# Eight small products side by side: state queries of a retention stage over four column tiles

## The chip, the cores and the metric

The kernel runs on one core of a Trainium2 chip. The metric is the time of one execution on the device in microseconds (us), the median of the runs shown. The engines in this document are TensorE (PE; its weight loads are listed apart as PEld), VectorE (DVE), ScalarE (ACT), GpSimd (POOL, which here mostly issues DMAs), and the queue of SyncE (SP), which issues the other DMAs.

## The reference, cut to what matters

One inference step of two decoder layers, for a prompt of 256 tokens and for a sample group of 8 batch entries with 4 tokens each. The second layer is a retention layer with 4 heads, keys of 256 and values of 512 elements. For the sample group each batch entry has a carried state of 4 heads x 256 x 512, which is read, used and written back:

```python
def retention_block(q, k, v, s_prev, log_g):
    ...
    o = jnp.einsum('bhij,bjhe->bihe', scores, v)
    q_decay = jnp.exp(log_g[None, :] * (i[:, None] + 1.0))
    o = o + jnp.einsum('bihd,bhde->bihe', q, s_prev) * q_decay[None, :, :, None]
    ...
    s_new = jnp.exp(log_g * L)[None, :, None, None] * s_prev + jnp.einsum('bjhd,bjhe->bhde', k * k_decay[None, :, :, None], v)
    return o, s_new
```

The second line of `o` is the query of the state (q times `s_prev`), and `s_new` is its update. The prompt goes through the same block in two chunks of 128 tokens for each head.

## The kernel before, in words

The retention stage has eight units. Unit n does two things at once. For the prompt it does head h = n // 2, chunk c = n % 2. For the sample group it does batch entry b = n: all of that entry's states, 2 MB, which are eight blocks (k = 0 to 7; head k // 2, half k % 2 of the 256 key rows) of 128 partitions x 512 values.

The program order is written out by hand for each engine, with semaphores between the engines. On PE (`pe_odd`) a unit is: the prompt's scores (into bank 5); state blocks 0 and 1; the S products of the prompt's key and value (banks 0 and 1); state blocks 2 and 3; scores times V (bank 6), and where c = 1 two more products with `qd` and S1; state blocks 4 to 7; and the four transposes of `rn`, for which PE waits until DVE has written `rn`. A state block (`sample_states`) is two products: the query, in which 32 columns of `QM` (the queries of all heads' sample tokens, zero outside this batch entry) meet the block and add to the 32 partitions of head h in bank 4 (`BN`), at column tile (0, 32 h); and the state product of `K4m` and `V4`, over the whole array, into bank 2 or 3 in turn. DVE then updates the block in place (`update`: decay times old state plus that bank).

On DVE a unit is: the scores' decay (`scr`), `qd` where c = 1, the gating of the unit before, updates 0 and 1, a rounding step of the unit before, updates 2 and 3, the two S2 steps where c = 1, update 4, the moments of bank 6, update 5, the reciprocal and the scaled rows (`rn`), and updates 6 and 7. ACT does a root between the moments and the reciprocal.

The states lie in the four slots of the weight ring `raw`, two to a batch entry (heads 0 and 1, heads 2 and 3, 1 MB each). So a slot goes round every two units: POOL stores half of entry n after update 3 or 7 (line 584), and the half of S2 where c = 1 (line 587); SP, whose queue is in order, waits for that store and loads the same half of entry n + 2 (line 303). PE waits for the half that a query reads (`SR_in`). When the stage is over PE goes on to the output projection, whose operands hang on the last `rn`.

The same column tiles are used in two other places: line 1179, four products of 512 columns ahead of the stage, one on each tile, and line 1268, the sample scores of cross-attention, eight products of 256 columns on four tiles.

Of the kernel before, what the change touches and what calls it, by code (L numbers as in the profile page):

```python
# [24 lines left out]
SEQ, DEC_B, DEC_T = 256, 8, 4  # L25
NS = DEC_B * DEC_T
# [10 lines left out]
RH, RDK, RDV = 4, 256, 512  # L37
# [26 lines left out]
def build(nc, a, outs):  # L64
# [31 lines left out]
    with ctx:  # L96
        def sb(name, shape, dt=F32, scope=ctx):
            return scope.enter_context(nc.sbuf_tensor(name, [P] + shape, dt))

        def sem(name):  # L100
            return ctx.enter_context(nc.semaphore(name))
# [98 lines left out]
        QM = sb("QM", [8, DEC_B * (NS + DEC_T)], F32, od)  # L200
# [25 lines left out]
        def state_slot(b, hp):  # L226


            return (G["out", 1].first + 2 + 2 * (b % 2) + hp) % 4

        def state(b, h):
            return raw[:, state_slot(b, h // 2), 4 * (h % 2):4 * (h % 2) + 4, :].rearrange("p (d x) n -> p d (x n)", d=2)
# [11 lines left out]
        ps = ctx.enter_context(nc.psum_tensor("ps", [P, 8, 512], F32))  # L244
        BN = 4
# [10 lines left out]
        def s(name):  # L256
            if name not in S:
                S[name] = sem(name)
            return S[name]
# [295 lines left out]
        def transpose(pe, out, x, rows=P):  # L555
            return pe.transpose(out, x, ident[0:rows, 0:rows])  # L556
# [305 lines left out]
        def dve_odd(dve, l):  # L862
# [77 lines left out]
            def update(b, k):  # L940

                dve.wait_ge(s("SU_ps"), 8 * b + k + 1)
                st = state(b, k // 2)[:, k % 2, :]
                dve.scalar_tensor_tensor(out=st, in0=st, scalar=gL(k // 2, DEC_T), in1=ps[:, 2 + k % 2, :],  # L944
                                         op0=ALU.mult, op1=ALU.add).then_inc(s("SR_new"), 1)
# [180 lines left out]
        def pe_odd(pe, l):  # L1126
            g = G["in", l]
            first_step(pe, g, 3 * l, normed, s("z_ready"), CREDIT)
            products(pe, g, normed, s("z_ready"), CREDIT, i0=1, i1=4)

            def naturals(i, idx):

                if idx or i == 4:
                    return
                for t in range(4):
                    e = 4 * (i - 5) + t
                    pe.wait_ge(s("v4T_ready"), e + 1)
                    if e >= 2:
                        pe.wait_ge(s("vR_ready"), e - 1)
                    bank = 5 + e % 2  # L1140
                    for c in range(2):
                        transpose(pe, ps[:, bank, c * P:(c + 1) * P], vt[:, t, c * P:(c + 1) * P])
                    transpose(pe, ps[:, bank, 2 * P:3 * P], v4T[:, t, :, :].rearrange("p r i -> p (r i)")).then_inc(s("vR_ps"), 1)
            for i in range(4, 9):
                products(pe, g, normed, s("z_ready"), CREDIT, i0=i, i1=i + 1, hook=naturals)

            products(pe, g, normed, s("z_ready"), CREDIT, i0=9, i1=10)
            pe.wait_ge(s("kdup"), 1)
            for h in range(RH):
                for dt in range(2):  # L1150
                    mm = pe.matmul(ps[0:64, 7, h * NS:(h + 1) * NS], k4T[:, 2 * h + dt, 0:2, :].rearrange("p r i -> p (r i)"),
                                   mT[:, 2 * h + dt, SEQ:T], start=dt == 0, stop=dt == 1)
            mm.then_inc(s("scS_ps"), 1)
            products(pe, g, normed, s("z_ready"), CREDIT, i0=10, i1=11)
            pe.wait_ge(s("k4T_full"), 1)
            pe.wait_ge(s("vR_ready"), 16)
            for r in range(2):
                for k in range(4):
                    tr = transpose(pe, ps[:, 5 + r, k * P:(k + 1) * P], k4T[:, 4 * r + k, :, :].rearrange("p r i -> p (r i)"))
                tr.then_inc(s("k4_ps"), 1)  # L1160

            def turn_keys(n):
                c, hf = divmod(n, 2)
                for k in range(4):
                    tr = transpose(pe, ps[:, KR_BANKS[n], k * P:(k + 1) * P], sq[:, 4 * hf + k, c * P:(c + 1) * P])
                tr.then_inc(s("kR_ps"), 1)

            def before_heads(i, idx):


                if idx:
                    return
                pe.wait_ge(s("K4_ready"), 2)
                pe.wait_ge(s("scS_ready"), 1)
                for n in range(3):
                    turn_keys(n)
                pe.wait_ge(root_ready, 2 * 3 * l + 1)
                for h in range(RH):
                    pe.matmul(ps[h * NS:(h + 1) * NS, BN, :], scS[0:64, h, :], V4[0:64, h * RDV:(h + 1) * RDV].bitcast(F32),
                              start=True, stop=False, skip_group_check=True, tile_position=(0, h * NS))  # L1180
            products(pe, g, normed, s("z_ready"), CREDIT, i0=11, i1=12, hook=before_heads)
            pe.wait_ge(s("kR_ready"), 3)
            turn_keys(3)

            def sample_states(b, tiles):

                for k in tiles:
                    h = k // 2
                    n = 8 * b + k
                    pe.wait_ge(s(f"SR_in{b % 2 * 2 + h // 2}"), 16 * (b // 2) + 16)  # L1190
                    pe.matmul(ps[h * NS:(h + 1) * NS, BN, :], QM[:, k, b * NS:(b + 1) * NS], state(b, h)[:, k % 2, :], start=False,  # L1191
                              stop=b == DEC_B - 1 and k % 2 == 1, skip_group_check=True, tile_position=(0, h * NS))
                    if k == 0:
                        pe.wait_ge(s("K4m_ready"), b + 1)
                    if n >= 2:
                        pe.wait_ge(s("SR_new"), n - 1)
                    pe.matmul(ps[:, 2 + k % 2, :], K4m[:, b % 2, k * P:(k + 1) * P], V4[:, h * RDV:(h + 1) * RDV],  # L1197
                              start=True, stop=True).then_inc(s("SU_ps"), 1)

            pe.wait_ge(s("z_ready"), CREDIT + 48)  # L1200
            pe.wait_ge(s("QM_step"), 3)

            for n, (h, c) in enumerate(UNITS):
                tok = slice(c * CHUNK, (c + 1) * CHUNK)
                if n:
                    pe.wait_ge(s("rs_ready"), n)
                for dt in range(2):
                    mm = pe.matmul(ps[:, 5, 0:P], sq[:, 2 * h + dt, tok], mT[:, 2 * h + dt, tok], start=dt == 0, stop=dt == 1)
                mm.then_inc(s("rs_ps"), 1)
                sample_states(n, (0, 1))  # L1210

                if n:
                    if c == 1:
                        pe.wait_ge(s("S1_ready"), h + 1)
                    else:
                        pe.wait_ge(s("S2_ready"), 2 * h)
                for dt in range(2):
                    pe.matmul(ps[:, dt, :], kR[:, c, h * RDK + dt * P:h * RDK + dt * P + P], vR[:, c, h * RDV:(h + 1) * RDV],
                              start=True, stop=True).then_inc(s("S_ps"), 1)
                sample_states(n, (2, 3))  # L1220
                pe.wait_ge(s("rs_ready"), n + 1)
                if n:
                    pe.wait_ge(s("rn_ready"), n)
                pe.wait_ge(s("kR_ready"), 4)
                mm = pe.matmul(ps[:, 6, :], scr[:, n % 2, :], vR[:, c, h * RDV:(h + 1) * RDV], start=True, stop=c == 0)
                if c == 1:
                    pe.wait_ge(s("qd_ready"), h + 1)
                    pe.wait_ge(s("S1_ready"), h + 1)
                    for dt in range(2):
                        mm = pe.matmul(ps[:, 6, :], qd[:, dt, :], S1[:, dt, :], start=False, stop=dt == 1)  # L1230
                mm.then_inc(s("ro_ps"), 1)
                sample_states(n, (4, 5, 6, 7))
                pe.wait_ge(s("rn_ready"), n + 1)
                if n:
                    pe.wait_ge(s("rg_ready"), n)
                for k in range(4):
                    tr = transpose(pe, ps[:, 7, k * P:(k + 1) * P], rn[:, k * P:(k + 1) * P])
                tr.then_inc(s("rT_ps"), 1)
            pe.wait_ge(s("rn_ready"), 9)
            pe.wait_ge(s("rg_ready"), 8)  # L1240
            for k in range(4):
                tr = transpose(pe, ps[:, 7, k * P:(k + 1) * P], rn[:, k * P:(k + 1) * P])
            tr.then_inc(s("rT_ps"), 1)
# [660 lines left out]
```

## Time and profile before

| what | value |
|---|---|
| median of 3 runs | 1332.78 us (1331.82 to 1333.16) |
| span of the profiled execution | 1330.2 us, from the first to the last instruction |
| PE busy | 1230.3 us, 92% of the span |
| DVE busy | 768.5 us, 58% |
| ACT busy | 584.4 us, 44% |
| moved by DMA | 233.64 MB, mean 176 GB/s |
| mean granted TensorE clock | 0.971 of full |

The profiled execution has no time of its own beside its span; the span lies 2.6 us below the median. Busy time is the sum of the instructions' durations without overlap, and matmuls that run together in one array count once. Durations of single instructions include the way through the array, so the start of the next instruction tells better what one costs.

### The profile page before, as it was taken

What the parts mean: (1) busy time and instruction counts of PE and PEld (TensorE: products, weight loads), DVE (VectorE), ACT (ScalarE), POOL (GpSimd) and SP (SyncE); (2) the same over time, 40 slices, a digit from 0 to 9 for tenths busy, and PEclk for the clock granted to TensorE, in tenths of its full rate; (3) what the DMA queues carried; (4) which work ended last, traced back from release to release, by engine and by line L of the source; (5) the groups of instructions that cost most, each with busy time, mean ns of one, the idle gap of its engine ahead of it and who ended that gap; (6) DMA issues with size and microseconds to landing.
All of it is one profiled execution on the core that took longest, in us unless ns stands there. A gap on an engine that the chain in (4) does not pass through costs nothing. (4 is left out here: it accounts for less than half of the span.)

```text
span 1330.2 us, 22925 instructions
## 1 busy us (share of the span) xinstructions
PE 1230.3 (92%) x8557; PEld 1091.7 (82%) x8557; DVE 768.5 (58%) x1020; ACT 584.4 (44%) x940; POOL 294.2 (22%) x521
## 2 busy tenths in 40 slices
PE   6999998887999999799999999899998779999995
PEld 4999897587999999699996333599996579999994
DVE  3585735227888733866555665447445167888433
ACT  5456534235655644423345111155434156556442
POOL 4001201114556510200000111003001125564402
PEclk9999999998999999799999999899999789999998
DMA  9647555632545355354444777748647324444440
GB/s 215 234 131 255 188 190 197 251 103 83 171 158 166 126 163 193 105 173 148 142 158 155 272 284 279 255 147 284 226 154 253 138 95 159 158 159 146 150 127 36
DMA packets 177267, 233.64 MB, mean 176 GB/s; under 512 B 5374, under 2 KB 153226, under 8 KB 177200
## 3 DMA queue, kind: packets, MB, share of 16 engines
q1 hardware_dynamic: 159088, 169.09, 39.2%
q0 software_dynamic: 18112, 63.60, 13.6%
q8 instruction: 48, 0.79, 0.2%
q14 instruction: 19, 0.16, 0.0%
HBM read 207.50 MB, written 25.16 MB: 175 GB/s over the span
## 5 line engine op out<-in xcount | busy, mean ns | idle before, releaser
L392 PE MATMUL ps<-hh,wh 128*128 128x288 f32 x1600 | 486.3, 304 | 34.8 <-DVE hl L450 28.2
L327 DVE TENSOR_TENSOR wl<-raw,wh 128x2048 fp32r<-128x2048 f32 (+2 forms) x154 | 331.7, 2154 | 313.4 <-ACT wh L324 313.3
L392 PE MATMUL ps<-hl,wh 128*128 128x288 f32 x1600 | 478.9, 299 | 0.0
L392 PE MATMUL ps<-hh,wl 128*128 128x288 f32 x1600 | 477.0, 298 | 0.0
L324 ACT ACTIVATE wh<-raw 128x2048 fp32r<-128x2048 f32 (+3 forms) x154 | 277.7, 1804 | 296.5 <-PE ps L392 288.0
L392 PEld LDWEIGHTS ps<-hh,wh 128*128 128x128 f32 x1600 | 306.1, 191 | 41.6 <-issue 33.8
L392 PEld LDWEIGHTS ps<-hh,wl 128*128 128x128 f32 x1600 | 308.0, 192 | 0.0
L392 PEld LDWEIGHTS ps<-hl,wh 128*128 128x128 f32 x1600 | 307.5, 192 | 0.3
L392 PE MATMUL ps<-aH,wh 128*128 128x288 f32 x352 | 104.2, 296 | 0.0
L392 PE MATMUL ps<-aL,wh 128*128 128x288 f32 x352 | 103.8, 295 | 0.0
L392 PE MATMUL ps<-aH,wl 128*128 128x288 f32 x352 | 103.6, 294 | 0.0
L458 POOL TENSOR_TENSOR mT<-mT,rstd 128x288 f32<-128x288 f32 x42 | 40.8, 1004 | 227.7 <-DVE rstd L433 227.7
L392 PE MATMUL ps<-wh,mh 128*128 128x256 f32 x256 | 73.4, 287 | 6.0 <-DVE wl L327 6.0
L584 POOL DMA_DIRECT2D out<-raw x16 | 12.2, 761 | 284.4 <-DVE raw L944 284.4
L392 PE MATMUL ps<-wl,mh 128*128 128x256 f32 x256 | 72.4, 283 | 0.0
L392 PE MATMUL ps<-wh,ml 128*128 128x256 f32 x256 | 72.4, 283 | 0.0
L944 DVE SCALAR_TENSOR_TENSOR raw<-raw,ps 128x512 f32<-128x512 f32 x64 | 43.6, 682 | 46.3 <-PE ps L1197 46.3
L1455 POOL TENSOR_TENSOR aL<-pd,aH 128x288 f32 (+1 forms) x44 | 68.6, 1578 | 4.2 <-ACT aH L1581 4.2
L1191 PE MATMUL ps<-raw,QM 128*32 128x512 f32 x128 | 66.9, 605 | 0.0
L392 PEld LDWEIGHTS ps<-aH,wl 128*128 128x128 f32 x352 | 66.3, 188 | 0.0
L392 PEld LDWEIGHTS ps<-aL,wh 128*128 128x128 f32 x352 | 66.1, 188 | 0.0
L392 PEld LDWEIGHTS ps<-aH,wh 128*128 128x128 f32 x352 | 66.0, 187 | 0.0
(286 smaller groups left out, 1682.3 us busy)
## 6 DMA issues: line engine op xcount, KB each, us to landing
raw<-w_ffn_up SPq DMA_DIRECT2D x44, 1024.0 KB, 5.0
raw<-w_in_odd SPq DMA_DIRECT2D x24, 1024.0 KB, 5.1
ring<-cache_mem_k POOLq DMA_DIRECT2D x16, 1024.0 KB, 5.4
ring<-cache_mem_v POOLq DMA_DIRECT2D x16, 1024.0 KB, 6.2
raw<-state_retention SPq DMA_DIRECT2D x16, 1024.0 KB, 5.2
out<-raw POOLq DMA_DIRECT2D x16, 1024.0 KB, 5.3
raw<-w_ffn_down SPq DMA_DIRECT2D x16, 768.0 KB, 4.4
raw<-w_in_even SPq DMA_DIRECT2D x10, 1024.0 KB, 6.7
```

The costliest lines, as they stand in the source:

```text
L324: e.activation(wh[:, c % 2, 0:kn, :], src, ACT.Copy).then_inc(hi_ready, 1)
L327: e.tensor_tensor(wl[:, c % 2, 0:kn, :], src, wh[:, c % 2, 0:kn, :].bitcast(F32), ALU.subtract).then_inc(lo_ready, 1)
L392: mm = pe.matmul(out, lhsT, rhs, start=(kc == 0 and n_k == 0 and n == 0), stop=(kc == g.nk - 1 and n_k == kn - 1 and n == 2))
L458: pool.tensor_tensor(mT[:, t, :], mT[:, t, :], rstd[:], ALU.mult).then_inc(scaled, 1)
L584: pool.dma_start(states_dram(ret_sample, n, half), states(n, half)).then_inc(s(f"SR_out{n % 2 * 2 + half}"), 16)
L944: dve.scalar_tensor_tensor(out=st, in0=st, scalar=gL(k // 2, DEC_T), in1=ps[:, 2 + k % 2, :], op0=ALU.mult, op1=ALU.add).then_inc(s("SR_ne ...
L1191: pe.matmul(ps[h * NS:(h + 1) * NS, BN, :], QM[:, k, b * NS:(b + 1) * NS], state(b, h)[:, k % 2, :], start=False, stop=b == DEC_B - 1 and ...
L1455: pool.tensor_tensor(aL[:, i * 2 + j, :], pd[:, j, :], aH[:, i * 2 + j, :].bitcast(F32), ALU.subtract).then_inc(s("a_lo"), 1)
```

## The change

A new helper issues the eight queries of a batch entry together, at the start of the unit, just behind the prompt's scores: first half 0 of the key rows for the four heads, one on each column tile, then half 1. PE waits for both halves of the entry's states ahead of them. The queries, and their waits, leave `sample_states`, which keeps the state products where they were. Update 0 of an entry waits on DVE for the last of the queries (`SQ_ps`), since it overwrites what they read.

```diff
             def update(b, k):
                 dve.wait_ge(s("SU_ps"), 8 * b + k + 1)
+                if k == 0:
+                    dve.wait_ge(s("SQ_ps"), b + 1)
...
+            def sample_rows_of(b):
+                for hp in range(2):
+                    pe.wait_ge(s(f"SR_in{b % 2 * 2 + hp}"), 16 * (b // 2) + 16)
+                for dt in range(2):
+                    for h in range(RH):
+                        k = 2 * h + dt
+                        mm = pe.matmul(ps[h * NS:(h + 1) * NS, BN, :], QM[:, k, b * NS:(b + 1) * NS], state(b, h)[:, dt, :], start=False,
+                                       stop=b == DEC_B - 1 and dt == 1, skip_group_check=True, tile_position=(0, h * NS))
+                mm.then_inc(s("SQ_ps"), 1)
...
                 for k in tiles:
                     h = k // 2
                     n = 8 * b + k
-                    pe.wait_ge(s(f"SR_in{b % 2 * 2 + h // 2}"), 16 * (b // 2) + 16)
-                    pe.matmul(ps[h * NS:(h + 1) * NS, BN, :], QM[:, k, b * NS:(b + 1) * NS], state(b, h)[:, k % 2, :], start=False,
-                              stop=b == DEC_B - 1 and k % 2 == 1, skip_group_check=True, tile_position=(0, h * NS))
...
                 mm.then_inc(s("rs_ps"), 1)
+                sample_rows_of(n)
                 sample_states(n, (0, 1))
```

## Rows read from the trace of the kernel before

**Rows 1.** The page, engines: busy us, share of the span, instructions.

```profile
PE 1230.3 (92%) x8557; PEld 1091.7 (82%) x8557; DVE 768.5 (58%) x1020; ACT 584.4 (44%) x940; POOL 294.2 (22%) x521
```

**Rows 2.** Stretches: the stage, a c = 0 unit, a c = 1 unit, each from rn to rn.

```profile
core 0: us, PE busy (x) PEld busy (x) DVE busy (x) ACT busy (x) POOL busy (x), PEclk, DMA share, GB/s
719.40:842.10 122.70, 122.70 (x311) 37.96 (x311) 73.34 (x130) 21.75 (x30) 14.22 (x19) 1.00 0.75 268
779.90:794.50 14.60, 14.60 (x39) 4.50 (x38) 8.34 (x16) 2.99 (x4) 1.53 (x2) 1.00 0.81 288
794.50:810.90 16.40, 16.40 (x43) 5.27 (x42) 9.96 (x20) 1.96 (x3) 2.21 (x3) 1.00 0.79 287
```

**Rows 3.** Groups of the stage by line: busy us, mean ns, idle before.

```profile
L1191 PE MATMUL ps<-raw,QM 128*32 128x512 f32 x128 | 66.9, 605 | 0.0
```

**Rows 4.** Timeline into a unit: start us, us, engine, line, operation.

```profile
780.40 0.50 PE L1197 MATMUL ps<-V,K4m 128*128 128x512 f32 x1
...
780.93 0.69 DVE L944 SCALAR_TENSOR_TENSOR raw<-raw,ps 128x512 f32<-128x512 f32 x1 [0.55 <-PE ps L1197]
...
781.71 1.05 PE L1191 MATMUL ps<-raw,QM 128*32 128x512 f32 x2
...
782.69 0.50 PE L1197 MATMUL ps<-V,K4m 128*128 128x512 f32 x1
```

**Rows 5.** Timeline of PE in a c = 1 unit, scores times V.

```profile
803.34 0.51 PE L1197 MATMUL ps<-V,K4m 128*128 128x512 f32 x1
803.68 1.02 PE L1225 MATMUL ps<-vR,scr 128*128 128x512 f32 x2
804.54 1.88 PE L1230 MATMUL ps<-S,qd 128*128 128x512 f32 x4
806.35 1.04 PE L1191 MATMUL ps<-raw,QM 128*32 128x512 f32 x2
```

**Rows 6.** Timeline of DVE in a c = 0 unit, from update 4 on.

```profile
791.50 0.69 DVE L944 SCALAR_TENSOR_TENSOR raw<-raw,ps 128x512 f32<-128x512 f32 x1 [1.65 <-PE ps L1197]
...
793.70 0.81 DVE L1021 TENSOR_SCALAR rn<-ps,small 128x512 f32<-128x512 f32 x1
```

**Rows 7.** Timeline of PE at lines 1179 and 1268, with what follows each.

```profile
710.58 1.06 PE L1179 MATMUL ps<-V,rowsn 64*32 64x512 f32 x8
711.57 0.40 PE L392 MATMUL ps<-hh,wh 128*128 128x288 f32 x1
...
1023.35 1.09 PE L1268 MATMUL ps<-kTb,qB 128*32 128x256 f32 x16
1024.37 0.48 PE L1284 MATMUL ps<-prT,vN 128*128 128x256 f32 x1
```

**Rows 8.** Timeline of DVE in unit 0: updates 0 and 1, update 4.

```profile
723.45 1.28 DVE L944 SCALAR_TENSOR_TENSOR raw<-raw,ps 128x512 f32<-128x512 f32 x2
...
729.22 0.69 DVE L944 SCALAR_TENSOR_TENSOR raw<-raw,ps 128x512 f32<-128x512 f32 x1 [1.65 <-PE ps L1197]
```

**Rows 9.** DMA issues (KB, us to landing), two in the timeline, a stretch.

```profile
raw<-state_retention SPq DMA_DIRECT2D x16, 1024.0 KB, 5.2
out<-raw POOLq DMA_DIRECT2D x16, 1024.0 KB, 5.3
...
723.36 0.38 SPq L303 DMA_DIRECT2D raw<-state_retention  x1
...
781.92 0.78 POOL L584 DMA_DIRECT2D out<-raw  x1 [6.29 <-DVE raw L944]
...
789.50:794.00 4.50, 4.50 (x11) 0.97 (x9) 2.78 (x7) 0.30 (x1) 0.75 (x1) 1.00 1.04 407
```

**Rows 10.** Stretches: idle PE after the stage, what follows, cross-attention of layer 0.

```profile
843.60:846.30 2.70, 0.01 (x1) 0.00 (x0) 2.63 (x7) 0.92 (x2) 0.78 (x1) 1.00 0.24 93
846.50:853.00 6.50, 4.72 (x20) 4.35 (x20) 1.81 (x4) 0.72 (x2) 0.71 (x1) 0.50 0.73 242
...
267.00:273.00 6.00, 2.63 (x34) 1.18 (x34) 0.17 (x1) 0.77 (x2) 0.00 (x0) 1.00 0.23 90
```

## The prediction

> **What bounds the kernel now.** The page comes first: TensorE (PE) is busy 92% of the span [rows 1], so nearly every stage ends when PE does, and time taken off PE in one stage is kept if nothing else in that stage takes its place. The stretches come next. The eight units of the retention stage fill 719.4 to 842.1; in them PE shows no idle time at the full clock, VectorE (DVE) works 73.3 of 122.7 us, and the DMA engines are at 0.75. One unit with c = 0 takes 14.6 us, one with c = 1 takes 16.4 [rows 2]. The groups say what PE does: 128 query records, two to a product, so 64 products [rows 3]. The timeline gives what a product really costs: query 781.71, its state product 782.69, so 0.98 us, during which three quarters of the array's columns have nothing to do [rows 4]. Eight are 7.84 us of a unit of 14.6. "Busy" hides that: the table counts a 32-column product as a whole one.
>
> **The eight products together.** They go in two rounds over the four column tiles. One 512-column float32 product takes 0.86 (803.68 to 804.54), two in a row 1.81 [rows 5]. The kernel already has this pattern twice: four 512-column products on the four tiles take from 710.58 to 711.57, 0.99 us, as much as one alone takes here; and the eight 256-column ones of cross-attention take 1.02 (1023.35 to 1024.37), two rounds of 0.43 and 0.16 for changing over [rows 7]. So I take 2 x 0.86 + 0.14 = 1.86 us. From below nothing beats four at once; from above, eight in turn are 8 x 0.86 + 0.14 = 7.0 (a rival below).
>
> The Trainium skill ("TensorE: Matmul & The Clock Gate", Part 3, measured speedup) has three 512-column products on three column tiles at 2.38 times one, not 3. An estimate by that page would be 8 x 0.86 / 3.17 + 0.14 = 2.3 us, 0.45 more in each of eight units, 3.5 us in all. The trace's 0.99 for four does not agree, and I keep the trace.
>
> **A unit without other limits.** I count from the end of the preceding unit's rn, the moment that lets PE go on. From PE's last step before it to the query is 1.31 (780.40 to 781.71, the rn transposes and the scores) [rows 4]; query 1.86, so the first state product (K4m) is at 3.17. K4m 1 follows about 0.23 later (512 columns in one pass; its update waits for update 0 anyway), the S products start 0.34 after that and take 1.81 [rows 5]: K4m 2 at 5.55, K4m 3 at 5.78, scores x V at 6.12 and 0.86 long: K4m 4 at 6.98. In a c = 1 unit the two qd products add 1.81 [rows 5]. Then DVE sets the pace: update 4 starts 0.53 after its product [rows 4], and from its start to the end of rn are 3.01 (791.50 to 793.70 + 0.81) [rows 6]. The unit is 6.98 + 0.53 + 3.01 = 10.52 (c = 0) or 12.33 (c = 1). Of the 7.84 only 1.86 stays, but the gain is 4.0 to 4.1 and not 6.0: the last four products were hidden for the most part behind update 4, the moments and the scaled rows.
>
> Sum: units 1 to 7 took 3 x 14.6 + 4 x 16.4 = 109.4 and would take 3 x 10.52 + 4 x 12.33 = 80.9, so 28.5 saved. Unit 0 starts late on DVE (update 0 at 723.45, after the weight split); from there K4m 2 and 3, scores x V and update 4 follow at 726.6 in place of 729.22 [rows 8]: 2.6 more. Together 31.1. What follows the last unit hangs on the same rn and comes earlier by as much.
>
> **The added waits.** DVE's wait for SQ_ps costs nothing: PE issues the query ahead of the K4m product for which DVE waits already. PE's wait moves: the second half of a batch entry's states was needed only at K4m 4, and is now needed ahead of everything. Behind it on PE stand the whole unit, and DVE's updates with it. For units 0 and 1 it costs nothing: the fourth and last of those loads is issued at 723.36 and lands some 5.2 us later, before the query of unit 1 at about 731 [rows 9]. For later ones: the slot is free when update 7 of two units earlier is done, stored and loaded over. Store 5.3, load 5.2 [rows 9], and 0.3 from the update (780.93 + 0.69) to the store's issue at 781.92 [rows 4, 9]. Two transfers at once move 407 GB/s [rows 9], so 1.05 MB are 2.58 us, and the other 2.6 of the 5.2 are latency, of which I put 2.2 ahead of the data (an estimate from these rows).
>
> I step through a pair from the query of an even unit, 0. Store of the first half: issued 6.4, data 8.6 to 11.2, landed 11.6; its reload's data from 13.8. Update 7 ends at 10.4 (rn at 10.52 - 1.31 = 9.2, then updates 6 and 7, some 1.2: two in a row take 1.28 [rows 8]), so the second half's store is issued at 10.7, has data from 12.9, shares with that reload, ends 17.15, lands 17.55; its reload has data from 19.8, and shares with the odd unit's first store (issued 10.5 + 6.4 = 16.9, data from 19.1) and the half-megabyte S store behind it: done at 24.95, landed 25.35. The next even query can run at 25.45; PE and DVE would be there at 10.52 + 12.33 = 22.85. A wait of 2.6 us ahead of units 2, 4 and 6, 8 us; odd units come out within 0.6. Without sharing it would be 0, with both shares full (2.58 each) 10.7 + 10.5 + 5.2 + 0.1 - 22.85 = 3.65, so 11. I take 8: 31.1 - 8 = 23.1.
>
> **The clock.** In the stage it is full [rows 2]. After the last unit PE had 2.7 us with nothing to do (843.6 to 846.3), and the granted clock then was 0.50 (1.2 GHz) to 853; while PE had 2.63 busy of 6.0 us in cross-attention it stayed at full [rows 10]. A wait of 2.6 looks like the first. Half clock over the query and the S products would add 1.7 each, 3.5 per wait, at most 10. I take a third, 3.
>
> The profiled execution's 1330.2 lies 2.6 under the median. 1332.8 - 23.1 + 3 = **1313**; on its own 1304 to 1321.
>
> **Rivals.**
> (a) The states are there in time. For it: the DMA engines have a quarter of the stage free [rows 2], and sharing is my estimate. Against it: eight megabytes of states and half of S (8.9 million bytes) a pair over 22.85 us are 390 GB/s, against 407 at best. 1332.8 - 31.1 = 1302.
> (b) PE, with pauses in every unit, runs much of the stage at half clock. Place: transposes, scores, query, S, scores x V, 1.2 (of the 1.31) + 1.86 + 1.81 + 0.86 = 5.7 us in a c = 0 unit and 7.5 in a c = 1 unit, which would double: 13.2 a pair, 53 over the stage. It eats the 23.1 when 44% of the stage is at half clock; at the whole, with the 8 us of waits still there, 1332.8 - 23.1 + 53 = 1363, at a third 1327. For it: the first two of [rows 10]. Against it: 2.63 of 6.0 busy was enough there, and a unit keeps more than that. The Trainium skill ("TensorE: Matmul & The Clock Gate", HAM oscillation) tells of this mechanism, bursts of products between waits for DMA that fall back to half clock. The trace agrees once [rows 10], and no row shows it in this stage.
> (c) The change doesn't do what it says: the products go in turn. The query is 7.0, a unit 5.1 longer than reckoned: 8 x 5.1 = 41 against 31.1, so about 1343 (the waits for states vanish). Against it stand both patterns of [rows 7].
>
> **Chances.** Forecast 0.65; (a) 0.13; (b) 0.17, half of it slower or the same; (c) 0.05. Two runs of this kernel can be told apart from about 0.2% (2.7 us). Faster: 0.65 + 0.13 + 0.09 = 0.87; the same 0.03; slower 0.10. The range takes in (a) and the milder part of (b): 1300 to 1326.
>
> **What would show it.** The query records in bursts of 16 within 1.9 us; PE idle ahead of them at units 2, 4 and 6, ended by the state loads, some 2.6 us; DMA share in the stage up from 0.75 to near 0.9; rn to rn some 22.9 us a pair where nothing waits and about 25.5 where states do, against 31.0; granted clock. Wrong it is if the bursts last nearer 7 us, if the clock is at half over much of the stage, or if a wait for states is 5 us and more.

## The result, and the profile after

The changed kernel takes 1325.4 us (median of 4 runs, 1320.78 to 1326.04) against 1332.97 of the kernel before; the ratio is 0.9935, 95% interval 0.9918 to 0.9953. So it is faster by 0.65%, by 7.6 us where 20 were expected: outside the forecast's own 1304 to 1321, and just inside the 1300 to 1326 that takes in the rivals. The profiled execution took 1325.95, with a span of 1324.2.

The page's engines and DMA issues of the changed kernel (busy us, share, instructions; KB each, median us to landing), which answer to [rows 1] and [rows 9]:

```profile
PE 1193.6 (90%) x8557; PEld 1094.7 (83%) x8557; DVE 766.3 (58%) x1020; ACT 584.3 (44%) x940; POOL 296.3 (22%) x521
...
raw<-state_retention SPq DMA_DIRECT2D x16, 1024.0 KB, 7.3
out<-raw POOLq DMA_DIRECT2D x16, 1024.0 KB, 6.2
```

PE lost 37 us of busy time, the span 6. A load of states now takes 7.3 us to land and not 5.2, a store 6.2 and not 5.3.

The stretches of the changed kernel, in the columns of [rows 2]: the stage from its first query to the last unit's rn, units 1 to 7 (from unit 0's rn to unit 7's), a c = 0 unit and a c = 1 unit from rn to rn, and the wait and the query inside that c = 1 unit.

```profile
core 0: us, PE busy (x) PEld busy (x) DVE busy (x) ACT busy (x) POOL busy (x), PEclk, DMA share, GB/s
720.60:835.30 114.70, 80.41 (x313) 35.07 (x312) 71.30 (x130) 21.75 (x30) 14.23 (x19) 0.85 0.83 290
730.70:835.30 104.60, 72.76 (x282) 32.18 (x282) 63.39 (x118) 15.76 (x23) 13.46 (x18) 0.84 0.86 301
774.70:784.70 10.00, 8.39 (x38) 3.88 (x38) 8.13 (x16) 2.99 (x4) 1.53 (x2) 1.00 0.84 304
754.30:774.70 20.40, 11.62 (x42) 4.91 (x42) 9.71 (x19) 1.96 (x3) 2.21 (x3) 0.75 0.86 300
755.50:762.20 6.70, 0.00 (x0) 0.00 (x0) 1.18 (x3) 1.67 (x2) 0.75 (x1) 0.51 0.99 345
762.30:765.70 3.40, 3.40 (x16) 0.62 (x16) 0.00 (x0) 0.00 (x0) 0.00 (x0) 0.50 0.88 305
```

A c = 0 unit went from 14.6 to 10.0 us, a c = 1 unit from 16.4 to 20.4. Inside the long one PE does nothing for 6.7 us while the DMA engines are busy throughout (0.99); the granted clock is then at 0.50, and the query that follows runs at half clock.

The same in the timeline of PE, first the query of the c = 0 unit and what follows it, then that of a c = 1 unit:

```profile
775.76 1.92 PE L1194 MATMUL ps<-raw,QM 128*32 128x512 f32 x16
777.62 0.73 PE L1207 MATMUL ps<-V,K4m 128*128 128x512 f32 x2
...
762.26 3.64 PE L1194 MATMUL ps<-raw,QM 128*32 128x512 f32 x16 [6.84 <-DMA raw<-state_retention]
765.84 0.73 PE L1207 MATMUL ps<-V,K4m 128*128 128x512 f32 x2
```

All eight products take 777.62 - 775.76 = 1.86 us at full clock, and 3.58 at half. The waits over the stage (us in total, times, longest) name what they hang on:

```profile
PE ps L1194 <- DMA raw<-state_retention: 19.1, 3, 6.8
```

Three waits, 6.84, 6.04 and 6.18 us, ahead of units 3, 5 and 7; none ahead of an even unit. Unit 1 has no wait either, but its query too runs at half clock (3.48 us to the next start):

```profile
731.79 3.55 PE L1194 MATMUL ps<-raw,QM 128*32 128x512 f32 x16
735.27 0.73 PE L1207 MATMUL ps<-V,K4m 128*128 128x512 f32 x2
```

### The profile page after: what moved, and what is told of

The parts are those of the page before. It is cut to its first block and busy times, and to the rows that moved or that the text cites. A ratio compares the mean times of both kernels' runs of the same rounds, so it can differ in the third digit from the quotient of the medians.

```text
span 1324.2 us, 22941 instructions
## 1 busy us (share of the span) xinstructions
PE 1193.6 (90%) x8557; PEld 1094.7 (83%) x8557; DVE 766.3 (58%) x1020; ACT 584.3 (44%) x940; POOL 296.3 (22%) x521
## 5 line engine op out<-in xcount | busy, mean ns | idle before, releaser
L1718 DVE SCALAR_TENSOR_TENSOR cb<-zb,cwT,cb 128x288 f32<-128x288 f32 x88 | 59.3, 712 | 0.8 <-ACT cb L1602 0.4
```

The costliest lines, as they stand in the source:

```text
L1718: dve.scalar_tensor_tensor(out=groups(cb[:, t, :]), in0=zb[:, t, :, 1:5], scalar=ftap(l, 1, tile), in1=groups(cb[:, t, :]), op0=ALU.mult, ...
```

## The experiments

Three theories of the lost time were set up after the result (their letters are not those of the rivals in the prediction). Theory A: the place of the wait. With both halves of the states due at the head of the unit, a ring of two entries is too short for the shorter units. Theory B: the DMA engines' throughput. Theory C: the half clock, with the waits a consequence. Code cuts are marked by "...".

**By key halves.** The slots hold key rows 0 to 127 and 128 to 255 of all heads, so that four queries on four column tiles need one slot. The cut shows it against the changed kernel.

```diff
-            return x[0, b, 2 * hp:2 * hp + 2].rearrange("h (d p) e -> p (h d) e", p=P)
+            return x[0, b, :, hp * P:(hp + 1) * P].rearrange("h p e -> p h e")
...
-                for hp in range(2):
-                    pe.wait_ge(s(f"SR_in{b % 2 * 2 + hp}"), 16 * (b // 2) + 16)
+                pe.wait_ge(s(f"SR_in{b % 2 * 2 + dt}"), 16 * (b // 2) + 16)
...
-                sample_rows_of(n)
+                sample_rows_of(n, 0)
                 sample_states(n, (0, 1))
...
+                sample_rows_of(n, 1)
                 sample_states(n, (4, 5, 6, 7))
```

The updates go over the four heads' first halves, then over the second ones.

> The eight queries are split into two groups of four, each still on all four column tiles: key rows 0 to 127 of all heads at the start of the unit, key rows 128 to 255 ahead of the fifth state product. The slots of the ring hold key halves in place of head pairs, so that each group waits for its own half of the states alone. Theory A (the one wait for both halves at the head of the unit makes the ring of two entries too short; the waits of 6.0 to 6.8 us ahead of units 3, 5 and 7 are its price): the second half is due some 5 to 6 us later in the unit, the 19.1 us of waits fall to 0 to 6, and with them most of the half clock; 1304 to 1312 us. Theory B (the DMA engines' throughput bounds the stage, 30.2 us a pair of units, wherever the waits stand): 1322 to 1327 us. Theory C (the half clock after thin stretches of TensorE is the price and the waits only follow from slower units): half clock in each odd unit stays, 1317 to 1322 us.

Measured: 1307.12 us (1305.92 to 1311.25), ratio 0.981 (0.9774 to 0.9846). Its stretches (unit 0's rn to unit 7's rn; a c = 0 unit; a c = 1 unit):

```profile
732.50:818.00 85.50, 72.07 (x282) 32.21 (x282) 63.34 (x118) 15.78 (x23) 13.45 (x18) 0.92 0.97 342
746.10:758.00 11.90, 9.99 (x38) 4.51 (x38) 8.16 (x17) 2.98 (x4) 1.53 (x2) 0.86 1.01 357
758.00:770.10 12.10, 10.18 (x42) 4.47 (x42) 9.71 (x20) 1.97 (x3) 2.21 (x3) 0.99 1.00 342
```

The timeline of PE in that c = 1 unit, the two groups of queries with what is ahead of each:

```profile
758.57 0.61 PE L1218 MATMUL ps<-mT,sq 128*128 128x128 f32 x4
759.11 1.06 PE L1194 MATMUL ps<-raw,QM 128*32 128x512 f32 x8
...
763.72 1.88 PE L1241 MATMUL ps<-S,qd 128*128 128x512 f32 x4
765.53 1.06 PE L1194 MATMUL ps<-raw,QM 128*32 128x512 f32 x8
```

Neither query waits; over the stage waits for states come to 0.8 us, once. A pair of units is 24.0 us where it was 30.4, with the same bytes, now at 342 GB/s over units 1 to 7 and not 301. That refutes B: 301 GB/s was not what the DMA engines could do. The half clock did not go away altogether (0.86 in the c = 0 unit).

**By head pairs.** The changed kernel once more; the slots stay; the queries come in two groups of two heads, each behind its own wait.

```diff
+                pe.wait_ge(s(f"SR_in{b % 2 * 2 + hp}"), 16 * (b // 2) + 16)
                 for dt in range(2):
-                    for h in range(RH):
+                    for h in (2 * hp, 2 * hp + 1):
```

> The slots stay as they are (heads 0 and 1, heads 2 and 3), and the queries come in two groups of four by head pair, each on two column tiles, each waiting for its own half of the states. A group is then two rounds of 0.86 and 0.14, so 3.7 us a unit in place of 1.86. Theory A: the waits go as in the run by key halves, and 0.9 us a unit more on the path (the second group, in part behind the updates): 1310 to 1320 us. Theory B: 1322 to 1327 us. If two column tiles do not run side by side, the query is 7 us and the time is above 1330.

Measured: 1319.09 us (1318.06 to 1319.92), ratio 0.9892 (0.986 to 0.9924), the upper end of theory A's range. No wait for states here either. Two column tiles give half of what four give: four products now take 1.84 us (746.59 to 748.43 in its trace), as long as eight took. A c = 0 unit is 12.1 us; a c = 1 unit is 15.4, and unit 3 of these has a granted clock of 0.89 on the mean, with half clock in its first query (2.98 us long). So a unit pays 2 us and more for the second group, and not the 0.9 expected.

**The wait alone.** The kernel before, with every query waiting for both halves.

```diff
-                    pe.wait_ge(s(f"SR_in{b % 2 * 2 + h // 2}"), 16 * (b // 2) + 16)
+                    for hp in range(2):
+                        pe.wait_ge(s(f"SR_in{b % 2 * 2 + hp}"), 16 * (b // 2) + 16)
```

> The kernel before, with nothing changed but that every query waits for both halves of its entry's states. Theory A: units of 14.6 and 16.4 us leave the slots some 4 us a unit more, so the states are there: within 2 us of 1333. If the wait for both halves costs whatever the length of a unit, some 5 us at three units: 1345 to 1350.

Measured: 1334.36 us (1331.17 to 1340.56, ten runs), ratio 1.0016 (0.9996 to 1.0036): no difference that can be told. The only wait for states in the stage is 0.2 us:

```profile
PE ps L1192 <- DMA raw<-state_retention: 0.2, 1, 0.2
```

In units of 14.6 and 16.4 us the early wait is free.

**A quarter of the transfers.** The changed kernel; each load and store of states carries one block of four, so three quarters of the carried states are neither read nor written.

```diff
-                    e.dma_start(states(b, hp), states_dram(a["state_retention"], b, hp)).then_inc(s(f"SR_in{b % 2 * 2 + hp}"), 16)
+                    e.dma_start(states(b, hp)[:, 0:1, :], states_dram(a["state_retention"], b, hp)[:, 0:1, :]).then_inc(s(f"SR_in{b % 2 * 2 + hp}"), 16)
...
-                    pool.dma_start(states_dram(ret_sample, n, half), states(n, half)).then_inc(s(f"SR_out{n % 2 * 2 + half}"), 16)
+                    pool.dma_start(states_dram(ret_sample, n, half)[:, 0:1, :], states(n, half)[:, 0:1, :]).then_inc(s(f"SR_out{n % 2 * 2 + half}"), 16)
```

> The changed kernel, in which each load and each store of states carries one block of four: three quarters of the carried states are neither read nor written. All waits stay. Theories A and B: the transfers are done in time, no wait ahead of the queries, stage shorter by 19 us of waits and by the half clock that they bring: 1300 to 1305 us. Theory C: half clock stays in every odd unit, 1308 to 1313 us. If the waits have another cause than the transfers: 1320 to 1326.

Measured: 1305.55 us (1302.54 to 1307.79), ratio 0.9782 (0.9749 to 0.9815). Stretches: unit 0's rn to unit 7's rn, a c = 0 unit, a c = 1 unit.

```profile
730.70:812.60 81.90, 69.08 (x282) 32.27 (x282) 63.44 (x119) 15.77 (x23) 10.55 (x18) 0.94 0.39 128
742.50:753.90 11.40, 9.71 (x38) 4.75 (x38) 8.20 (x17) 2.98 (x4) 1.11 (x2) 0.87 0.25 86
753.90:765.70 11.80, 9.84 (x42) 4.64 (x42) 9.73 (x19) 1.97 (x3) 1.80 (x3) 1.00 0.45 144
```

No wait for states is left, so the waits hang on the transfers. Units 1 to 7 take 81.9 us, where the forecast had 80.9 for units without other limits. That the two are so close is in part luck: the units are shorter than forecast, and half clock makes up for it. It comes here too, once in a pair, in the even units and with no wait ahead of it, so C has a part of its own; it costs 1.3 to 1.6 us each time (11.4 to 11.7 against 10.05) and not the whole gain.

**Even entries by a quarter.** As before, but only the even entries' transfers are cut; the odd entries, which PE waits for, keep theirs.

```diff
+                    few = slice(0, 4 if b % 2 or b < 2 else 1)
+                    e.dma_start(states(b, hp)[:, few, :], states_dram(a["state_retention"], b, hp)[:, few, :]).then_inc(s(f"SR_in{b % 2 * 2 + hp}"), 16)
...
+                    few = slice(0, 4 if n % 2 else 1)
+                    pool.dma_start(states_dram(ret_sample, n, half)[:, few, :], states(n, half)[:, few, :]).then_inc(s(f"SR_out{n % 2 * 2 + half}"), 16)
```

> The changed kernel, in which the states of the even batch entries from 2 on are loaded, and those of all even entries stored, by one block of four (the other three blocks are neither read nor written); the odd entries, ahead of which the waits stand, keep their full transfers. If the waits come from transfers that share the DMA engines (7 to 10 us in place of 5.2): the chain of an odd entry alone is update 7, 0.3, store 5.3, load 5.2, which is there before the query at 22.9 us, so no wait of more than 0.5 us, 1302 to 1309 us. If the odd entry's own chain of store and load is too long whatever else runs: 4 to 6 us of wait each remain, 1317 to 1325 us.

Measured: 1318.49 us (1317.22 to 1319.22), ratio 0.9894 (0.9879 to 0.9909). The waits:

```profile
PE ps L1196 <- DMA raw<-state_retention: 8.7, 3, 3.5
```

From 19.1 to 8.7, so over half of the wait went with the even entries' transfers, which had shared the DMA engines with those of the odd ones. The rest stayed. The time lies in the second expectation's range, but the waits (1.8, 3.4 and 3.5 us) lie between the two: neither "no more than 0.5" nor "4 to 6" came true. In its last pair the query of unit 5 starts at 784.69, the store behind update 7 is issued at 799.24, its reload at 806.96, and the query of unit 7 starts at 812.44: 14.55, 7.7 and 5.5 us, where the forecast's terms give 12.5, 5.3 and 5.2. The store overlaps the reload of the same entry's other half (issued at 798.19), and the unit's query ran at half clock (3.64 us long).

**Filling the wait.** The changed kernel with five more products, used by nothing, ahead of the queries of units 3, 5 and 7.

```diff
+                if b >= 3 and b % 2:
+                    for _ in range(5):
+                        pe.matmul(ps[:, 6, :], kR[:, 0, 0:P], vR[:, 0, 0:RDV], start=True, stop=True)
```

> The changed kernel with five more full products (512 columns, float32, result used by nothing) on TensorE ahead of the queries of units 3, 5 and 7, in the time in which it would wait for states. Theory C at its size: the queries behind the waits run at full clock, 1.85 in place of 3.6 us, and since the next store hangs on them, 1.7 us come back at each of three units: about 1320 us. If the half clock costs nothing because the transfers decide anyway: 1325. If the fill itself delays the query: above 1326.

Measured: 1321.99 us (1316.34 to 1322.68), ratio 0.9906 (0.9883 to 0.9929). The fill and the query of unit 3:

```profile
758.69 5.80 PE L1191 MATMUL ps<-vR,kR 128*128 128x512 f32 x10
764.42 1.92 PE L1197 MATMUL ps<-raw,QM 128*32 128x512 f32 x16
```

That query is back at 1.92, and the time near what theory C's size asks for; but the interval overlaps with the changed kernel's, and the half clock did not go: it came in the even units, in unit 2 behind a wait of 3.3 us that was not there before:

```profile
745.88 3.64 PE L1197 MATMUL ps<-raw,QM 128*32 128x512 f32 x16 [3.33 <-DMA raw<-state_retention]
```

Ahead of units 3 and 5 no wait is left behind the fill, so the fill itself may set when those queries start. The run settles nothing about the price of the half clock.

**Key halves with a fill.** The version by key halves, with 256-column products, used by nothing, in PE's short waits for updates late in each unit.

```diff
+                    for _ in range({6: 1, 7: 2}.get(k, 0)):
+                        pe.matmul(ps[:, 5, P:P + 256], kR[:, 0, 0:P], vR[:, 0, 0:256], start=True, stop=True)
                     if n >= 2:
                         pe.wait_ge(s("SR_new"), n - 1)
```

> The version by key halves (1307 us) with three more 256-column products of 0.43 us, result used by nothing, ahead of the state products 6 (one) and 7 (two) of each unit, where TensorE waits for VectorE. There the granted clock falls once a pair of units (3.4 us at half). If the fill keeps it full: 1.7 us less at three or four units, 1300 to 1303 us. If the clock falls all the same: 1306 to 1309. If the fill runs past the wait and delays the state products: above 1309.

Measured: 1305.91 us (1304.92 to 1310.0), ratio 0.9803 (0.9786 to 0.982). Unit 0's rn to unit 7's rn:

```profile
730.80:814.20 83.40, 75.47 (x324) 36.40 (x324) 63.44 (x119) 15.79 (x23) 13.48 (x18) 1.00 0.96 352
```

The clock is full throughout, and units 1 to 7 are 2.1 us shorter than by key halves alone; but the totals can't be told apart, and the time is not in the 1300 to 1303 expected with a full clock. Waits for states came back:

```profile
PEld ps L1194 <- DMA raw<-state_retention: 7.8, 7, 1.8
```

Seven of them, 7.8 us in all, took what the clock gave. With the DMA engines busy at 0.96 they are probably the next bound at this length of unit; no run tested it.

**The early wait put back.** The version by key halves, with both waits at the head of the unit and nothing else moved.

```diff
-                pe.wait_ge(s(f"SR_in{b % 2 * 2 + dt}"), 16 * (b // 2) + 16)
+                if dt == 0:
+                    for hp in range(2):
+                        pe.wait_ge(s(f"SR_in{b % 2 * 2 + hp}"), 16 * (b // 2) + 16)
```

> The version by key halves (1307 us) with one thing moved: TensorE waits for both halves of the states at the head of the unit, as the change does; the two groups of queries, the slots and the transfers stay where they are. If the place of the wait is the cause (theory A): waits of some 5 to 7 us come back at every other unit and the half clock with them, 1320 to 1326 us. If the version by key halves gained through its slots, its order of updates or its two groups: within 3 us of 1307.

Measured: 1327.47 us (1318.0 to 1330.98), ratio 0.996 (0.9943 to 0.9978). In the profiled execution, the fastest of six, PE waits ahead of unit 2:

```profile
749.11 1.94 PE L1196 MATMUL ps<-raw,QM 128*32 128x512 f32 x8 [3.00 <-DMA raw<-state_retention]
```

All its waits for states in the stage are these:

```profile
PE ps L1196 <- DMA raw<-state_retention: 5.5, 3, 3.0
```

The time is as theory A wants, a little above its 1320 to 1326. By the medians the place of the wait by itself is worth some 20 us, with the queries, the slots and the transfers left alone; the kernel before took 1332.8 us beside the one version and 1332.7 beside the other. Its mechanism is only in part as expected. In the profiled execution, which is 11 us above that of the version by key halves, the waits are 3.0, 2.1 and 0.4 us ahead of the even units, and not 5 to 7. Units 1 to 7 are 13.5 us longer there, and their mean granted clock is 0.81 against 0.92, so most of this loss is not in the waits themselves; how much of it is half clock was not measured apart. The slower executions have no trace.

## Why the prediction was right and wrong

Right: the price of the eight products (1.86 forecast and measured), the units without other limits (10.5 and 12.3 forecast; 10.0 to 10.2 and 11.8 measured, the latter with a quarter of the transfers), unit 0 (2.6 forecast; from 719.43 to 732.23 before and 720.63 to 730.69 after, 2.7), DVE as what sets the pace of the second half, the added DVE wait at nothing, and that states would be late and the clock fall with it, though not ahead of the even units, where the forecast had both. The estimate of 2.3 us for the products, by the Trainium skill ("TensorE: Matmul & The Clock Gate", Part 3), differs from the 1.86 measured, and the measurement decides.

Wrong: the step from one pair to the next, "odd units come out within 0.6", for which the prediction shows no working, and with it the place and the size of the wait. The waits of over 6 us ahead of odd units are what the prediction itself named as the sign of being wrong ("5 us and more"). For units 1 to 7, from rn to rn:

| term | forecast | after |
|---|---|---|
| units without other limits | 80.9 | 3 x 10.1 + 4 x 11.8 = 77.5 |
| waits for states | 8 | 19.1 (6.84 + 6.04 + 6.18) |
| half clock | 3 | 8.0 (what is left) |
| sum | 91.9 | 104.6 (before: 109.8) |

What is left goes to the half clock, because unit 1, without a wait, took 13.4 us against 11.8 with a quarter of the transfers; in units 5 and 7 the half clock lasted longer, and from the query to rn they took 12.9 and 13.1 us against 12.3 in unit 1.

I followed the chain of an even entry, whose unit is short: its last store is issued 10.7 us after its query. In an odd unit it is 12.5 by the same terms (10.7 and the 1.81 of the two qd products), so store and reload at the undisturbed 5.3 and 5.2 end 23.0 us after the query, against 22.85 of a pair: every delay of a transfer there goes into the wait in full. And the delays were larger. I let two transfers share; the short even unit that follows without a wait puts both its stores on the queues while the odd entry's store and reload are under way. From the query of unit 5 to that of unit 7 the rows are (query, store, reload, query):

```profile
791.92 3.64 PE L1194 MATMUL ps<-raw,QM 128*32 128x512 f32 x16 [6.04 <-DMA raw<-state_retention]
...
806.42 0.78 POOL L584 DMA_DIRECT2D out<-raw  x1 [4.25 <-DVE raw L946]
...
813.79 0.38 SPq L303 DMA_DIRECT2D raw<-state_retention  x1
...
822.21 3.64 PE L1194 MATMUL ps<-raw,QM 128*32 128x512 f32 x16 [6.18 <-DMA raw<-state_retention]
```

The steps are 14.5 (791.92 to the store's issue at 806.42), 7.4 (to the reload at 813.79) and 8.4 (to the query at 822.21), 30.3 us; so the store is 2.1 late, the reload 3.2, and the unit itself 2.0, most of it the half clock. The upper bound that I gave for the wait, 3.65, held only for two transfers at a time, and for one of the two chains.

The half clock was mis-sized as well, 3 us for about 8: it came in every odd unit, in unit 1 without any wait, and it feeds the wait, since the next store hangs on the unit that it slows. The stretch of [rows 10] in which the clock stayed full was no argument against it: with a quarter of the transfers the clock fell to half for a part of the even units (0.87 on the mean) with no wait for states at all. Rival (a) is what the kernel does when the states are there, by a quarter of the transfers or, but for a few us, by key halves; rival (c) is refuted; of rival (b) the mechanism is there, at about 8 of the 53 us that it priced, not counting what it adds to the waits. That the 1325 measured lies beside rival (b)'s 1327, for a third of the stage at half clock, is luck: the mean clock of the stage was 0.85, but about half of its half clock fell in the waits, in which PE had nothing to do.

The rest of the difference lies outside these units: the first query starts 1.2 us later than before, and from the last unit's rn to the end it is 0.9 us longer. Neither looks like an effect of the change, since in the traces of the other runs that start lies between 719.3 and 721.7 and that end takes 486.6 to 493.3 us (488.9 here), but no run was made for it.

What stays open: why runs of one kernel differ by up to 13 us with the early wait (1318.0 to 1331.0). Perhaps it settles differently from run to run which transfers meet; that was not tried. Open too is how the time lost with the early wait divides between the waits and the half clock that comes with them.

## What to carry to other kernels

Packing small products onto the four column tiles paid nearly in full here (eight in 1.86 us, where eight full ones at 0.86 are 6.9), but grouping them also moves the earliest moment at which each operand is due; cost that deadline against the ring's turn-around, for the longest unit in the cycle and with all transfers in flight that the shorter units will then issue. Split the operands so that one group needs one buffer: four tiles by key halves kept the four products side by side and the late deadline, and took 1307 us where the change took 1325. When a wait grows, look at the clock behind it too.

## What the runs showed of the hardware

Eight 512-column float32 products of 32 columns each take 1.86 us on the four column tiles, about as long as two full ones in a row (1.81 in [rows 5]). In the changed kernel's long wait, with several transfers under way, the DMA engines were busy at 0.99 but moved 345 GB/s, not the 407 of [rows 9]; 1 MB loads of that run took up to 10.1 us to land. The granted clock fell to half in units where PE only paused for DVE (a quarter of the transfers, no wait for states), and in the version by key halves, where it fell once a pair, three small idle-time products a unit kept it full (1.00 over units 1 to 7 against 0.92).
